# Turning the FFN's gated product with VectorE blocks and a round trip through device memory

## The chip, the cores and the metric

The kernel runs on one core of a Trainium2 chip. The metric is the device time of one execution in microseconds (us). TensorE (PE) multiplies, VectorE (DVE) and ScalarE (ACT) do elementwise work, GpSimd (POOL) has its own instruction queue, and SyncE (SP) issues the loads. Each queue can issue DMAs. The data lie in SBUF (128 partitions) and in PSUM, where TensorE writes.

## What is computed

The program is two transformer-like blocks for 256 tokens of width 2048, all in fp32. The change touches only the feed-forward part (FFN) of the first block:

```
h2 = rms_norm(x, g_pre_ffn[l]) * (1 + scale_f) + shift_f
f = (jax.nn.silu(h2 @ w_ffn_gate[l]) * (h2 @ w_ffn_up[l])) @ w_ffn_down[l]
x = x + gate_f * rms_norm(f, g_post_ffn[l])
```

`w_ffn_gate` and `w_ffn_up` are 2048 x 5632, `w_ffn_down` is 5632 x 2048. Each fp32 factor is split into a high part (rounded to the type fp32r) and a low part (the rest), and a product is the sum of three matmuls, high by high, low by high and high by low.

## The kernel before, in words

**Units and the ring.** All weights stream as *units* of 128 x 1024 fp32 (512 KB): two blocks of 128 rows by 512 columns. SP loads a unit into one of four slots of `raw`. ScalarE writes its high part to `hi` (line 572), VectorE its low part to `lo` (line 1157); both have four slots. TensorE uses a unit in 12 matmuls of 128 x 512 (lines 2002 to 2004). Semaphores tie the four: SP may refill a slot of `raw` after VectorE's `unit_split`, ScalarE may write the slot of `hi` for unit u after TensorE has finished unit u-4 (`unit_used`), and TensorE waits for `unit_split`. Each engine runs a fixed list, written by hand: in each block the call `split(n)` means "n more units of the ring", and what stands between two such calls is done there. ScalarE and VectorE may thus be up to four units ahead of TensorE.

**The FFN.** Units are counted from `FFN0` here. For each of 11 hidden tiles (512 columns of the hidden layer, `FT`) there is a *gate tile* of 8 units (accumulated in PSUM banks 0 and 1 of `acc`, one for each half of 128 tokens) and an *up tile* of 8 units (banks 2 and 3). So tile n has gate units 16n to 16n+7 and up units 16n+8 to 16n+15. When a gate tile is done, ScalarE writes its silu to `sgt` (`read_out`, line 613). When the up tile is done, VectorE multiplies it with `sgt` into `tok` (line 1726), with tokens on partitions. The down projection needs the product with hidden columns on partitions. So TensorE turns it: after unit 2 of the next gate tile (`after={1: hidden}`) it makes 8 transposes of 128 x 128 with `ident` into the PSUM banks `tb` 0 and 1 (`transpose_tok`, `transpose_pair`, line 2084), ScalarE takes the high part from there to `hidh` (`take_hi`, line 590) and VectorE the low part to `hidl` (line 1283). The turned product of the last tile is made in the same way, after unit 2 of the first down tile, by `last_hidden`, which also turns `fG` (one transpose, line 2120).

**The down projection** has 4 tiles of 22 units. Its first tile uses `hidh` and `hidl` in order of the hidden columns. Units 20 and 21 need the eleventh hidden tile (`before={FK // 2 - 2: split_now}`).

**Late modulation blocks.** During the first units of the FFN (8 to 71) the ring also carries 32 blocks of a modulation matrix, one behind every second unit, which VectorE alone uses (`late_unit`, lines 1191 and 1193). In that stretch three loads of 512 KB go through the ring for every two units.

GpSimd does a few small operations early in the program and issues no DMA. Two short DMAs on ScalarE's queue (`store_gate`, `load_gate`) carry `fG` through `gate_rows` in device memory.

Of the kernel before, what the change touches and what calls it, by code (L numbers as in the profile page):

```python
# [43 lines left out]
FT = FFN // N  # L44
# [158 lines left out]
def two_blocks(nc, x_in, fm_in, row_in, table_in, mask1_in, mask2_in, pool_in, ws_in, kidx_in,  # L203
               wa, wb, wc, out):
    with ExitStack() as ctx:
        def sem(name):
            return ctx.enter_context(nc.semaphore(name))
# [88 lines left out]
        macc_tok = sb("macc_tok", [P, UNIT], at=tok_at + TT * N * 4)  # L296
        gate_row = sb("gate_row", [KD, P])
        gate_rows = nc.dram_tensor("gate_rows", (2, KD, P), F32, kind="Internal").ap()
        end1 = top[0]
        z = sb("z", [P, TT, D], at=x_at)  # L300

# [66 lines left out]
        tr_split = sem("tr_split")  # L368
        tr_hi = sem("tr_hi")
        tr_copy = sem("tr_copy")  # L370
        u_turned = sem("u_turned")
        u_taken = sem("u_taken")
        pool_split = sem("pool_split")
# [63 lines left out]
        def part_at(part, tt):  # L437

            if part < 2:
                return k_part[:, part, tt, :]  # L440
            if part < 4:
                return v[:, tt, (part - 2) * N:(part - 1) * N]
            return z[:, tt, (part - 4) * N:(part - 3) * N]

        block = ctx.enter_context(nc.Block())

# [74 lines left out]
        @block.gpsimd  # L521
        def _(pool):
            pool.memset(ones[:], 1.0).then_inc(memory_set, 1)

            pool.wait_ge(row_loaded, 4 * 16)
            pool.memset(kT2[:], 0.0).then_inc(memory_set, 1)

            pool.affine_select(out=wsT[:], in_=wsT[:], compare_op=ALU.is_ge, fill=0.0, base=0,
                               pattern=[[0, 8], [1, P]], channel_multiplier=-1).then_inc(ws_ready, 1)

            pool.wait_ge(rstd_ready, 3)
            for tt in range(TT):
# [12 lines left out]
            pool.tensor_tensor(kr[:, :, ih:IROPE], kn[:, :, 0:ih], iropeS[:, :, ih:IROPE], ALU.mult)  # L545
            pool.tensor_copy(kd[:, :, IROPE:IDIM], kn[:, :, IROPE:IDIM])
            pool.tensor_tensor(kd[:, :, 0:IROPE], kn[:, :, 0:IROPE], iropeC[:], ALU.mult).then_inc(kn_step, 1)
            pool.wait_ge(kn_step, 4)
            pool.tensor_tensor(kd[:, :, 0:IROPE], kd[:, :, 0:IROPE], kr[:], ALU.add).then_inc(kn_step, 1)
            pool.tensor_scalar(kx[:, :, IDIM:], kx[:, :, IDIM:], IDX_SCALE, None, ALU.mult)  # L550
            pool.wait_ge(kn_step, 5)
            pool.tensor_copy(kd[:, :, IDIM:], kd[:, :, 0:IDIM]).then_inc(kidx_ready, 1)

# [4 lines left out]
        def _(act):  # L558
# [39 lines left out]
            def take_hi_tile(dst, k, gain=None):  # L598
                for b in range(2):
                    act.wait_ge(tr_split, c.up("split"))  # L600
                    take_hi(dst, k + 2 * b, b, gain and (lambda j, b=b: gain(2 * b + j)))
# [308 lines left out]
            for k in range(4, KD // 2):  # L910
                take_scaled(k)
                split(1)
            def hidden(n, first=8):
                split(first)
                tile_done()
                read_out(lambda tt: sgt[:, tt, :], 0, ACT.Silu)
                split(8)
                take_hi_tile(hidh, n * 4)

            hidden(0, FFN0 + 12 - c.n["unit"])  # L920
            for n in range(1, FFN_MOD):
                hidden(n)
            with c.loop(act, FT - FFN_MOD, unit=16, raw=16, split=2) as n:
                hidden(n + FFN_MOD)
            store_gate(1)
            split(4)
            load_gate(gm2, 1)
            for t in range(3):
                split(FK // 2 - (5 if t == 0 else 1))
                square_tile(t % 2, t)  # L930
                if t == 0:

                    load_root()
                split(1)
# [201 lines left out]
        def _(dve):  # L1136
# [581 lines left out]
                split(1)  # L1718


            def hidden(n, units=16):
                split(units - 2)
                tile_done(2)
                for tt in range(TT):

                    dve.tensor_tensor(tok[:, 0, tt, :], acc[:, 2 + tt, :], sgt[:, tt, :], ALU.mult).then_inc(acc_free[2 + tt], 1)
                split(2)
                take_lo_tile(hidl, hidh, n * 4)

            hidden(0, FFN0 + 20 - c.n["unit"])  # L1730
            for n in range(1, FFN_MOD):
                hidden(n)
            add_bias(GATE_F, KD)
            gated_gain(GATE_F, "g_post_ffn")
            with c.loop(dve, FT - FFN_MOD, unit=16, raw=16, hi=2) as n:
                hidden(n + FFN_MOD)
            for t in range(3):
                split(FK // 2 - (t == 0))
                gated_tile(fmix, gm2, t % 2, t * N)
            split(FK // 2 - RING + 1)  # L1740
            base_of(slice(0, TT))
# [241 lines left out]
        def _(pe):  # L1983
# [434 lines left out]
            keep_warm(0, 3, mergedh, mergedl)  # L2418

            def next_hidden():  # L2420
                def hidden():

                    read_out(1)
                    transpose_tok(0, tr_split)

                tile(Hh, Hl, 0, 8, after={1: hidden})
                tile(Hh, Hl, 1, 8)

            tile(Hh, Hl, 0, 8, before={k: (lambda k=k: pe.wait_ge(*split_by[k])) for k in range(KD // 2)},
# [1 line left out]
            tile(Hh, Hl, 1, 8)  # L2431
            for n in range(FFN_MOD - 1):
                next_hidden()
            with c.loop(pe, FT - FFN_MOD, unit=16, raw=16, acc0=1, acc1=1, tb0=1, tb1=1):
                next_hidden()

            def last_hidden():
                read_out(1)
                transpose_tok(0, tr_split)
                gate_rows_out(1)  # L2440

            for t in range(4):
                if t == 0:
                    tile(hidh, hidl, 0, FK // 2, before={FK // 2 - 2: split_now}, after={1: last_hidden})
                elif t < 3:
                    tile(hidh, hidl, t % 2, FK // 2)
                else:
                    tile_by_halves(hidh, hidl, 1, FK // 2)
# [259 lines left out]
```

## Time and profile before

| | |
|---|---|
| median of 3 runs | 2390.59 us (2390.33 to 2390.76) |
| the profiled execution's own time | 2391.39 us |
| its span in the trace | 2389.7 us |
| granted TensorE clock, mean | 0.999 of full speed |
| PE, DVE, ACT, POOL busy | 99%, 68%, 47%, 0% of the span |

The profile comes from one execution. Its own time stands 0.80 us above the median of the runs, and 1.7 us above its span. TensorE is busy from end to end; matmuls overlap in the trace, each lasting longer than its step, so its busy share says that it is occupied but not how fast. Times in the trace are counted from the start of the span.

### The profile page before, as it was taken

Reading aid. Unit: us, or ns where it says so; the run is one execution under the profiler, and the core shown is the slowest. Engines: PE = TensorE matmul, PEld = TensorE weight load, DVE = VectorE, ACT = ScalarE, POOL = GpSimd, SP = SyncE. Lnnn points to the kernel's source line nnn. Section 1 sums busy time; section 2 is a strip of 40 time slices with the busy share of each in tenths; the row PEclk is TensorE's granted clock in tenths of the full one; section 3 lists DMA queues with packets and bytes.
Section 4 is the critical chain, followed back from the end, with each engine's and each line's share of the span. In section 5 each row is a group of like instructions: output and inputs, shape, how many; then the busy total and the mean of one; then the engine's idle time right before and its main releaser. Section 6 shows DMA issues by size and latency. Waiting matters only on the chain.

```text
span 2389.7 us, 31107 instructions
## 1 busy us (share of the span) xinstructions
PE 2373.9 (99%) x10995; PEld 1967.1 (82%) x10995; DVE 1614.6 (68%) x1994; ACT 1120.6 (47%) x1415; POOL 9.8 (0%) x18
## 2 busy tenths in 40 slices
PE   9999999999999999999999999999999999999998
PEld 7888788888888888888888888888888888888887
DVE  7998899899787765445444465666655557777664
ACT  4544545544464444444444454445544444444554
POOL 0001000000000000000000000000000000000000
PEclk9999999999999999999999999999999999999999
DMA  9986479999857875555555556655555554444454
GB/s 392 386 314 207 152 261 353 332 340 365 308 201 259 288 252 180 196 190 185 210 193 194 194 174 204 210 203 184 193 194 193 177 195 158 151 165 157 157 189 158
DMA packets 148490, 538.54 MB, mean 225 GB/s; under 512 B 16896, under 2 KB 18208, under 8 KB 147744
## 3 DMA queue, kind: packets, MB, share of 16 engines
q1 hardware_dynamic: 145584, 528.28, 63.2%
q10 hardware_dynamic: 2800, 8.81, 1.0%
q8 instruction: 71, 1.16, 0.2%
q14 instruction: 35, 0.29, 0.0%
HBM read 534.91 MB, written 2.11 MB: 225 GB/s over the span
## 4 chain that ended last, share of the span: by engine, by line
PE 97%; DVE 1%; DMA 1%; ACT 0%; issue 0%; SPq 0%; ACTq 0%; DVEq 0%
PE acc L2002 29%; PE acc L2004 29%; PE acc L2003 29%; PE tb L2084 2%; PE tb L2534 1%; DMA start_raw<-in_wa_dram 1%; PE tb L2002 1%; PE tb L2004 0%; PE tb L2003 0%; PE acc L2054 0%; PE acc L2053 0%; PE acc L2052 0%; PE tb L2537 0%; PE tb L2271 0%; PE acc L2063 0%
## 5 line engine op out<-in xcount | busy, mean ns | idle before, releaser
L1157 DVE TENSOR_TENSOR lo<-raw,hi 128x1024 fp32r<-128x1024 f32 x809 | 968.8, 1208 | 593.4 <-ACT hi L572 590.2
L572 ACT ACTIVATE hi<-raw 128x1024 fp32r<-128x1024 f32 x809 | 842.6, 1049 | 912.4 <-PE acc L2004 722.1
L2002 PE MATMUL acc<-hi,Hh 128*128 128x512 f32 x1960 | 775.5, 396 | 1.2 <-DVE Hl L1700 0.7
L2004 PE MATMUL acc<-hi,Hl 128*128 128x512 f32 x1960 | 764.3, 390 | 0.0
L2003 PE MATMUL acc<-lo,Hh 128*128 128x512 f32 x1960 | 763.1, 389 | 0.0
L2002 PEld LDWEIGHTS acc<-hi,Hh 128*128 128x128 f32 x1960 | 368.1, 188 | 79.2 <-issue 4.6
L2004 PEld LDWEIGHTS acc<-hi,Hl 128*128 128x128 f32 x1960 | 367.8, 188 | 77.9
L2003 PEld LDWEIGHTS acc<-lo,Hh 128*128 128x128 f32 x1960 | 368.3, 188 | 75.6 <-issue 1.4
L2002 PE MATMUL acc<-hi,hbh 128*128 128x512 f32 x512 | 204.7, 400 | 0.0
L2004 PE MATMUL acc<-hi,hbl 128*128 128x512 f32 x512 | 200.1, 391 | 0.0
L2003 PE MATMUL acc<-lo,hbh 128*128 128x512 f32 x512 | 199.6, 390 | 0.0
L2002 PE MATMUL acc<-hi,hidh 128*128 128x512 f32 x336 | 130.8, 389 | 0.0
L2004 PE MATMUL acc<-hi,hidl 128*128 128x512 f32 x336 | 130.7, 389 | 0.0
L2003 PE MATMUL acc<-lo,hidh 128*128 128x512 f32 x336 | 130.7, 389 | 0.0
L1193 DVE SCALAR_TENSOR_TENSOR macc<-late_raw,fm,macc 128x1024 f32<-128x1024 f32 x90 | 114.9, 1277 | 0.4
L2004 PEld LDWEIGHTS acc<-hi,hbl 128*128 128x128 f32 x512 | 96.1, 188 | 20.6
L2003 PEld LDWEIGHTS acc<-lo,hbh 128*128 128x128 f32 x512 | 96.4, 188 | 18.5
L2002 PEld LDWEIGHTS acc<-hi,hbh 128*128 128x128 f32 x512 | 96.3, 188 | 18.1
L2004 PEld LDWEIGHTS acc<-hi,hidl 128*128 128x128 f32 x336 | 63.1, 188 | 13.2
L2003 PEld LDWEIGHTS acc<-lo,hidh 128*128 128x128 f32 x336 | 63.1, 188 | 13.0
L2002 PEld LDWEIGHTS acc<-hi,hidh 128*128 128x128 f32 x336 | 63.1, 188 | 13.0
L1330 DVE SCALAR_TENSOR_TENSOR macc<-start_raw,fm,macc 128x1024 f32<-128x1024 f32 x45 | 57.5, 1278 | 0.1
(338 smaller groups left out, 1970.5 us busy)
## 6 DMA issues: line engine op xcount, KB each, us to landing
raw<-in_wa_dram SPq DMA_DIRECT2D x680, 512.0 KB, 4.3
late_raw<-in_wa_dram SPq DMA_DIRECT2D x96, 512.0 KB, 5.4
raw<-in_wb_dram SPq DMA_DIRECT2D x96, 512.0 KB, 4.2
start_raw<-in_wa_dram SPq DMA_DIRECT2D x64, 512.0 KB, 7.7
raw<-in_wc_dram SPq DMA_DIRECT2D x64, 512.0 KB, 3.5
x<-in_x_dram SPq DMA_DIRECT2D x2, 1024.0 KB, 6.1
gm<-gate_rows ACTq DMA_DIRECT2D x2, 1024.0 KB, 9.0
x<-in_x_dram ACTq DMA_DIRECT2D x1, 2048.0 KB, 9.3
```

Source lines behind the costliest of these rows:

```text
L572: act.activation(hi[:, s, 0:n], raw[:, r, 0:n], ACT.Copy).then_inc(hi_ready, 1)
L1157: dve.tensor_tensor(lo[:, s, 0:n], raw[:, r, 0:n], hi[:, s, 0:n].bitcast(F32), ALU.subtract)\
L1193: ins = dve.scalar_tensor_tensor(dst, w, vec("c", kt), dst, ALU.mult, ALU.add)
L1330: ins = dve.scalar_tensor_tensor(dst, start_raw[s][:], vec("c", kt), dst, ALU.mult, ALU.add)
L2002: pe.matmul(dst(tt), a, hi[:, s, w], start=first and i == 0, stop=False)
L2003: pe.matmul(dst(tt), a, lo[:, s, w], start=False, stop=False)
L2004: mm = pe.matmul(dst(tt), b, hi[:, s, w], start=False, stop=last and i == kts - 1)
L2084: ins = pe.transpose(tb[:, b, j * T + tt * P:j * T + (tt + 1) * P], src(tt, j), ident[:])
L2534: pe.matmul(tb[:, g // 2, (g % 2) * T:(g % 2 + 1) * T], q(g, P, P), k(T), start=True, stop=True)
```

## The change

TensorE's 88 transposes of the gated product go, and so do ScalarE's and VectorE's reads of `tb`. In their place:

1. VectorE, right behind the product, transposes it in 32 x 32 blocks (two instructions, one for each half of the tokens) from `tok` into `sgt`, whose silu is spent by then. The blocks are so placed that partition 32i+c holds block row c of token block i.
2. GpSimd stores the 512 KB of `sgt` to the new device tensor `hid_rows`, waits until that has landed, and reads it back in four DMAs of 32 partitions x 4 x 256 elements (128 KB each) into `tok`. The moves between groups of 32 partitions happen in these reads. Every run of bytes is 4 KB in the store and 1 KB in the reads.
3. ScalarE makes `hidh` from `tok` (`hidden_hi`) late in the next gate tile: behind its split of unit 16n+27, ahead of that gate tile's silu. VectorE makes `hidl` (`hidden_lo`) behind its split of the same unit.
4. For the last tile both happen at unit 12 of the first down tile. TensorE waits there for `hid_split` ahead of unit 0 (for the tenth tile) and ahead of unit 20 (for the eleventh).

The transpose of `fG` stays. The diff, cut to its core:

```
+            for n in range(FT):
+                pool.wait_ge(hid_blocks, n + 1)
+                pool.dma_start(hid_rows[:, :, :], blocks_out).then_inc(hid_stored, 16)
+                pool.wait_ge(hid_stored, 16 * (n + 1))
+                for j in range(4):
+                    pool.dma_start(blocks_in[32 * j:32 * j + 32, :, :], hid_rows[:, j, :].rearrange("(i c) m -> c i m", i=4))\
+                        .then_inc(hid_turned, 16)
...
-            def hidden(n, first=8):
-                split(first)
+            def hidden_hi(n, turned):
+
+                act.wait_ge(hid_turned, turned)
+                for tt in range(TT):
+                    act.activation(hidh[:, cols(n * 4, 4), tt * P:(tt + 1) * P].rearrange("p k (i t) -> p k i t", i=4),
+                                   turned_half(tt), ACT.Copy).then_inc(hid_hi, 1)
+
+            def hidden(n, turned):
+                split(16)
+                hidden_hi(n, turned)
                 tile_done()
                 read_out(lambda tt: sgt[:, tt, :], 0, ACT.Silu)
-                split(8)
-                take_hi_tile(hidh, n * 4)
...
+            def hidden_lo(n, taken):
+
+                for tt in range(TT):
+                    dve.wait_ge(hid_hi, taken + tt + 1)
+                    at = slice(tt * P, (tt + 1) * P)
+                    four = lambda ap: ap.rearrange("p k (i t) -> p k i t", i=4)
+                    ins = dve.tensor_tensor(four(hidl[:, cols(n * 4, 4), at]), turned_half(tt),
+                                            four(hidh[:, cols(n * 4, 4), at].bitcast(F32)), ALU.subtract)
+                ins.then_inc(hid_split, 1)
+
+            def hidden(units=6):
+                split(units)
                 tile_done(2)
                 for tt in range(TT):
-
                     dve.tensor_tensor(tok[:, 0, tt, :], acc[:, 2 + tt, :], sgt[:, tt, :], ALU.mult).then_inc(acc_free[2 + tt], 1)
-                split(2)
-                take_lo_tile(hidl, hidh, n * 4)
...
+                for tt in range(TT):
+                    ins = dve.transpose(blocks_out[:, :, tt * P:(tt + 1) * P].rearrange("p j (k t) -> p j k t", k=4),
+                                        tok[:, 0, tt, :].rearrange("p (k j c) -> p j k c", k=4, j=4))
+                ins.then_inc(hid_blocks, 1)
+                split(10)
...
-                def hidden():
-
-                    read_out(1)
-                    transpose_tok(0, tr_split)
-
-                tile(Hh, Hl, 0, 8, after={1: hidden})
+                tile(Hh, Hl, 0, 8)
                 tile(Hh, Hl, 1, 8)
...
-                    tile(hidh, hidl, 0, FK // 2, before={FK // 2 - 2: split_now}, after={1: last_hidden})
+                    tile(hidh, hidl, 0, FK // 2, before={i: (lambda n=n: pe.wait_ge(hid_split, n)) for i, n in ((0, FT - 1), (FK // 2 - 2, FT))},
+                         after={1: lambda: gate_rows_out(1)})
```

How the lists of the engines change shows at three places. The numbers at a row's start are the engine's count of instructions, and waits stand in brackets. First TensorE behind unit 2 of the second gate tile, before the change:

```order
2960 L2003 MATMUL acc<-lo,Hh 128x512
2961 L2004 MATMUL acc<-hi,Hl 128x512
2962 L2084 MATMUL tb<-ident,tok 128x128 [waits tb_free0,acc_free3,acc_free2]
2963 L2084 MATMUL tb<-ident,tok 128x128 x3
2964 L2084 MATMUL tb<-ident,tok 128x128 [waits tb_free1]
2965 L2084 MATMUL tb<-ident,tok 128x128 x3
2966 L2002 MATMUL acc<-hi,Hh 128x512 [waits unit_split]
```

With the change the rows of line 2084 are gone there, and the matmuls of the next unit follow directly. Next VectorE, from the product of the first hidden tile on, before:

```order
755 L1726 TENSOR_TENSOR tok<-acc,sgt 128x512 [waits unit_used]
756 L1726 TENSOR_TENSOR tok<-acc,sgt 128x512
757 L1193 SCALAR_TENSOR_TENSOR macc_end<-raw,fm,macc_end 128x1024 [waits raw_loaded3,unit_split]
758 L1157 TENSOR_TENSOR lo<-raw,hi 128x1024 [waits hi_ready] x2
759 L1283 TENSOR_TENSOR hidl<-tb,hidh 128x512 [waits tr_hi] x2
760 L1193 SCALAR_TENSOR_TENSOR macc_end<-raw,fm,macc_end 128x1024 [waits raw_loaded2,unit_split]
761 L1157 TENSOR_TENSOR lo<-raw,hi 128x1024 [waits hi_ready] x2
```

and VectorE at the same place with the change:

```order
755 L1767 TENSOR_TENSOR tok<-acc,sgt 128x512 [waits unit_used]
756 L1767 TENSOR_TENSOR tok<-acc,sgt 128x512
757 L1773 STREAM_TRANSPOSE sgt<-tok 128x4x128 [waits acc_free3,acc_free2]
758 L1773 STREAM_TRANSPOSE sgt<-tok 128x4x128
759 L1225 SCALAR_TENSOR_TENSOR macc_end<-raw,fm,macc_end 128x1024 [waits raw_loaded3,unit_split]
760 L1189 TENSOR_TENSOR lo<-raw,hi 128x1024 [waits hi_ready] x2
761 L1225 SCALAR_TENSOR_TENSOR macc_end<-raw,fm,macc_end 128x1024 [waits raw_loaded2,unit_split]
762 L1189 TENSOR_TENSOR lo<-raw,hi 128x1024 [waits hi_ready] x2
```

The two transposes now stand directly behind the product, and the low part (`hidl`) has moved ten units down, to instruction 769. Last, ScalarE at the end of the second gate tile with the change (the silu `sgt<-acc` stood there before too, and `hidh` eight units further up):

```order
431 L593 ACTIVATE hi<-raw 128x1024 [waits unit_used,raw_loaded0]
432 L593 ACTIVATE hi<-raw 128x1024 [waits unit_used,raw_loaded1]
433 L938 ACTIVATE hidh<-tok 128x4x128 [waits hid_turned]
434 L938 ACTIVATE hidh<-tok 128x4x128
435 L634 ACTIVATE sgt<-acc 128x512 [waits unit_used]
436 L634 ACTIVATE sgt<-acc 128x512
437 L593 ACTIVATE hi<-raw 128x1024 [waits unit_used,raw_loaded3]
```

ScalarE's wait for the four reads (`hid_turned`) now stands ahead of the silu and of the split of the next unit.

## Rows read from the trace of the kernel before

**Rows 1.** The page: busy time by engine.
```profile
PE 2373.9 (99%) x10995; PEld 1967.1 (82%) x10995; DVE 1614.6 (68%) x1994; ACT 1120.6 (47%) x1415; POOL 9.8 (0%) x18
```

**Rows 2.** The page: chain that ended last, share of the span by line.
```profile
PE acc L2002 29%; PE acc L2004 29%; PE acc L2003 29%; PE tb L2084 2%; PE tb L2534 1%; DMA start_raw<-in_wa_dram 1%; PE tb L2002 1%; PE tb L2004 0%; PE tb L2003 0%; PE acc L2054 0%; PE acc L2053 0%; PE acc L2052 0%; PE tb L2537 0%; PE tb L2271 0%; PE acc L2063 0%
```

**Rows 3.** Two stretches of the FFN: busy us and counts, clock, DMA share, GB/s.
```profile
core 0: us, PE busy (x) PEld busy (x) DVE busy (x) ACT busy (x) POOL busy (x), PEclk, DMA share, GB/s
688.00:863.00 175.00, 175.00 (x793) 145.19 (x792) 124.56 (x116) 75.16 (x81) 0.00 (x0) 1.00 0.80 277
863.00:1164.00 301.00, 301.00 (x1358) 249.66 (x1357) 148.55 (x138) 127.91 (x136) 0.00 (x0) 1.00 0.57 194
```

**Rows 4.** PE timeline around the transposes of the second hidden tile: start, duration, engine, line.
```profile
766.92 0.39 PE L2004 MATMUL acc<-hi,Hl 128*128 128x512 f32 x1
767.15 1.03 PE L2084 MATMUL tb<-ident,tok 128*128 128x128 f32 x8
767.94 0.48 PE L2002 MATMUL acc<-hi,Hh 128*128 128x512 f32 x1
768.26 0.40 PE L2003 MATMUL acc<-lo,Hh 128*128 128x512 f32 x1
768.49 0.39 PE L2004 MATMUL acc<-hi,Hl 128*128 128x512 f32 x1
```

**Rows 5.** PE timeline, last hidden tile, with the transpose of fG.
```profile
1163.49 0.39 PE L2002 MATMUL acc<-hi,hidh 128*128 128x512 f32 x1
...
1168.71 0.40 PE L2004 MATMUL acc<-hi,hidl 128*128 128x512 f32 x1
1168.94 1.04 PE L2084 MATMUL tb<-ident,tok 128*128 128x128 f32 x8
...
1169.84 0.48 PE L2002 MATMUL acc<-hi,hidh 128*128 128x512 f32 x1
1170.16 0.40 PE L2003 MATMUL acc<-lo,hidh 128*128 128x512 f32 x1
1170.39 0.39 PE L2004 MATMUL acc<-hi,hidl 128*128 128x512 f32 x1
```

**Rows 6.** All groups of PE, by shape: busy us, mean ns, idle before.
```profile
L2084 PE MATMUL tb<-ident,tok 128*128 128x128 f32 x400 | 51.9, 272 | 0.7 <-DVE tok L1275 0.7
```

**Rows 7.** VectorE timeline from the second product on, idle time in brackets.
```profile
761.91 1.29 DVE L1726 TENSOR_TENSOR tok<-acc,sgt 128x512 f32<-128x512 f32 x2 [1.21 <-PE acc L2004]
...
768.42 1.29 DVE L1283 TENSOR_TENSOR hidl<-tb,hidh 128x512 fp32r<-128x512 f32 x2 [1.76 <-ACT hidh L590]
769.62 1.27 DVE L1193 SCALAR_TENSOR_TENSOR macc_end<-raw,fm,macc_end 128x1024 f32<-128x1024 f32 x1
770.82 2.35 DVE L1157 TENSOR_TENSOR lo<-raw,hi 128x1024 fp32r<-128x1024 f32 x2
```

**Rows 8.** ScalarE timeline at the end of the second gate tile.
```profile
742.58 1.07 ACT L572 ACTIVATE hi<-raw 128x1024 fp32r<-128x1024 f32 x1 [0.34 <-DMA raw<-in_wa_dram]
743.54 1.06 ACT L613 ACTIVATE sgt<-acc 128x512 f32<-128x512 f32 x2
746.40 1.06 ACT L572 ACTIVATE hi<-raw 128x1024 fp32r<-128x1024 f32 x1 [1.80 <-DMA raw<-in_wa_dram]
```

**Rows 9.** Instructions that write or read tok: ns min/median/max, first and last start.
```profile
L1275 DVE TENSOR_TENSOR tok<-tok,sgt x44: 413/682/694, 210.8 to 2199.2; 128x512 f32<-128x512 f32 x40, 128x256 f32<-128x256 f32 x4
L1010 ACT ACTIVATE x<-tok x8: 617/625/635, 1638.6 to 1707.8; 128x512 f32 x8
```

**Rows 10.** The page: DMA issues, KB each, median us from issue to landing.
```profile
raw<-in_wa_dram SPq DMA_DIRECT2D x680, 512.0 KB, 4.3
late_raw<-in_wa_dram SPq DMA_DIRECT2D x96, 512.0 KB, 5.4
start_raw<-in_wa_dram SPq DMA_DIRECT2D x64, 512.0 KB, 7.7
```

**Rows 11.** Waits in the stretch 688 to 1164 us: total us, times, longest.
```profile
ACT hi L572 <- PE acc L2004: 143.5, 93, 2.2
ACT hi L572 <- DMA raw<-in_wa_dram: 85.7, 53, 4.2
```

More of the change, by code:

```diff
@@ L298, in two_blocks @@
         gate_rows = nc.dram_tensor("gate_rows", (2, KD, P), F32, kind="Internal").ap()
+        hid_rows = nc.dram_tensor("hid_rows", (P, 4, TT * P), F32, kind="Internal").ap()
         end1 = top[0]
@@ L370, in two_blocks @@
         tr_copy = sem("tr_copy")
+        hid_blocks = sem("hid_blocks")
+        hid_stored = sem("hid_stored")
+        hid_turned = sem("hid_turned")
+        hid_hi = sem("hid_hi")
+        hid_split = sem("hid_split")
         u_turned = sem("u_turned")
@@ L443, in part_at, with turned_half @@
             return z[:, tt, (part - 4) * N:(part - 3) * N]
+        blocks_out = sgt[:].rearrange("p a (j m) -> p (a j) m", j=2)
+        blocks_in = tok[:, 0].rearrange("p a (i m) -> p (a i) m", i=2)
+        def turned_half(tt):
+            return blocks_in[:, :, tt * P:(tt + 1) * P].rearrange("p i (k t) -> p k i t", k=4)
         block = ctx.enter_context(nc.Block())
@@ L912, in _ @@
                 split(1)
-            def hidden(n, first=8):
-                split(first)
+            def hidden_hi(n, turned):
[6 more added lines that the diff above has]
+                hidden_hi(n, turned)
                 tile_done()
                 read_out(lambda tt: sgt[:, tt, :], 0, ACT.Silu)
-                split(8)
-                take_hi_tile(hidh, n * 4)
[L920 to L924, printed above, removed]
+            split_to(FFN0 + 12)
+            tile_done()
+            read_out(lambda tt: sgt[:, tt, :], 0, ACT.Silu)
+            for n in range(FFN_MOD - 1):
+                hidden(n, 64 * (n + 1))
+            with c.loop(act, FT - FFN_MOD, unit=16, raw=16) as n:
+                hidden(n + (FFN_MOD - 1), n * 64 + 64 * FFN_MOD)
+            split(8)
             store_gate(1)
@@ L927, in _ @@
             load_gate(gm2, 1)
+            split(4)
+            hidden_hi(FT - 1, 64 * FT)
             for t in range(3):
-                split(FK // 2 - (5 if t == 0 else 1))
+                split(FK // 2 - (9 if t == 0 else 1))
                 square_tile(t % 2, t)
@@ L1718, in _ @@
                 split(1)
-            def hidden(n, units=16):
-                split(units - 2)
+            def hidden_lo(n, taken):
[8 more added lines that the diff above has]
+                split(units)
                 tile_done(2)
@@ L1726, in hidden @@
                     dve.tensor_tensor(tok[:, 0, tt, :], acc[:, 2 + tt, :], sgt[:, tt, :], ALU.mult).then_inc(acc_free[2 + tt], 1)
-                split(2)
-                take_lo_tile(hidl, hidh, n * 4)
-            hidden(0, FFN0 + 20 - c.n["unit"])
+                n = c.up("hidden")
+                for tt in range(TT):
+                    dve.wait_ge(acc_free[2 + tt], n + (TILES_BEFORE_OUT // 2 + 3))
+                for tt in range(TT):
+                    ins = dve.transpose(blocks_out[:, :, tt * P:(tt + 1) * P].rearrange("p j (k t) -> p j k t", k=4),
+                                        tok[:, 0, tt, :].rearrange("p (k j c) -> p j k c", k=4, j=4))
+                ins.then_inc(hid_blocks, 1)
+                split(10)
+            hidden(FFN0 + 18 - c.n["unit"])
             for n in range(1, FFN_MOD):
-                hidden(n)
+                hidden_lo(n - 1, TT * (n - 1))
+                hidden()
             add_bias(GATE_F, KD)
             gated_gain(GATE_F, "g_post_ffn")
-            with c.loop(dve, FT - FFN_MOD, unit=16, raw=16, hi=2) as n:
-                hidden(n + FFN_MOD)
+            with c.loop(dve, FT - FFN_MOD, unit=16, raw=16, hidden=1) as n:
+                hidden_lo(n + (FFN_MOD - 1), n * TT + TT * (FFN_MOD - 1))
+                hidden()
+            hidden_lo(FT - 1, TT * (FT - 1))
             for t in range(3):
-                split(FK // 2 - (t == 0))
+                split(FK // 2 - (9 if t == 0 else 0))
                 gated_tile(fmix, gm2, t % 2, t * N)
@@ L2433, in _ @@
                 next_hidden()
-            with c.loop(pe, FT - FFN_MOD, unit=16, raw=16, acc0=1, acc1=1, tb0=1, tb1=1):
+            with c.loop(pe, FT - FFN_MOD, unit=16, raw=16, acc0=1, acc1=1):
                 next_hidden()
[L2437 to L2440, printed above, removed]
             for t in range(4):
                 if t == 0:
-                    tile(hidh, hidl, 0, FK // 2, before={FK // 2 - 2: split_now}, after={1: last_hidden})
+                    tile(hidh, hidl, 0, FK // 2, before={i: (lambda n=n: pe.wait_ge(hid_split, n)) for i, n in ((0, FT - 1), (FK // 2 - 2, FT))},
+                         after={1: lambda: gate_rows_out(1)})
                 elif t < 3:
```

## Prediction

> **What bounds the kernel now.** I read the page first. TensorE is busy for 99% of the span, VectorE for 68%, ScalarE for 47%, GpSimd for almost nothing [rows 1]. The chain of waits that ended last runs through the matmuls of the weight stream (lines 2002 to 2004, 29% each), and the transposes of line 2084, those of every stage together, hold 2% of it [rows 2]. So nothing but TensorE's own list sets the end, and an instruction taken off that list is worth its step in the list, as long as no wait takes its place. Then I read the FFN by stretches [rows 3]: full clock in both, TensorE without a gap, DMA queues 80% busy while the late modulation blocks share the ring (688 to 863 us) and 57% afterwards. VectorE works 124.56 of 175 us in the first. Last I read timelines around one hidden tile for the steps and the leads.
>
> **A step of TensorE.** From the first matmul at 1163.49 to the one at 1168.71 there are 23 steps [rows 5], so a matmul costs 0.227 us of TensorE's time although each lasts 0.39, and a unit of 12 costs 2.72 us.
>
> **What is removed.** In the second hidden tile the last matmul ahead of the transposes starts at 766.92, and the second behind them at 768.26 [rows 4]. That is 1.34 us where two steps would be 0.45. The 8 transposes cost 0.89 us, 0.11 each. In the last tile the same distance is 1168.71 to 1170.16, 1.45 us, with the transpose of fG among them [rows 5]: 1.00 us for nine, again 0.11 each. All 11 tiles: 11 x 0.89 = **9.8 us**. Bounds: fG's transpose stays and is alone now; if it then costs a whole duration (0.272 us by the mean in [rows 6]) and not 0.11, the gain is 9.6. The busy time in [rows 6] gives 51.9 / 400 = 0.130 us for one transpose, and 88 of them 11.4 us, the upper end. I take 9.8, since it is the measured distance between matmuls. The Trainium skill (VectorE: DVE Perf Modes, The three transpose paths) puts TensorE's 128x128 transpose at 390 ns, measured in bf16, and its rules for kernel authors say to turn 128x128 on TensorE when PSUM will do; by that figure the estimate would be 34.3 us gained, and by that rule no change of this kind. The trace disagrees with the figure as a price: transposes overlap, and only the step is paid.
>
> **What is added to VectorE.** Two block transposes of 128 x 512 behind the product. No row shows one; the nearest is an operation of the same size in SBUF, 0.682 us [rows 9], so 1.36 us for both, between 0.82 (two of the 0.413 of half the size) and 2.4 (two like the split of 1024 columns, 2.35 for a pair [rows 7]). The low part stays two operations (1.29 before [rows 7], 1.36 from SBUF). Four tiles add some 6 us to the 124.56 of 175 in the busiest stretch [rows 3]. It is hidden by VectorE's lead. That lead is least right here: unit 34 starts at 767.94 and is 0.09 us longer than 2.72 [rows 4], so TensorE starts unit 36 at 773.5. Its low part is the first of the two that start at 770.82, and ends at 772.0 [rows 7]. The lead is 1.5 us, because both engines stood for the transposes (VectorE idle for 1.76 us, and its 1.29 us of work). This stop goes away, and the 1.36 us of block transposes come in its place. So the least lead should grow, not shrink. If the cover were gone, four tiles by 1.36 us would be 5.4 us.
>
> **What is added to ScalarE.** The high part from SBUF: two of 0.625 us [rows 9] ahead of the silu. Before, ScalarE stood idle 1.80 us after that silu, waiting for a weight load [rows 8]; the 1.25 us fit in it. The split of the next unit does not move. VectorE's low part delays the modulation block behind it by about 1.3 us and so refills that ring slot later; the lead takes it.
>
> **What is added to the queues.** GpSimd issues five DMAs for each tile; nothing is queued behind them but the next tile's. SP's list is unchanged. Each tile moves 1.05 MB more. At 277 GB/s for a share of 0.80 [rows 3] the queues do 346 GB/s when full, so this is 3.0 us of their time. In some 10 us of such a trip they have 2.0 us to spare in the first stretch, so the loads fall behind by about 1.0 us, or 2.5 if the reads cost double for their runs of 1 KB. Afterwards the share is 0.57 and there is room.
>
> **When the turned tile lands.** Call T the end of an up tile. The product starts at once and takes 1.29 us [rows 7], the transposes 1.36. Store: a load of the same 512 KB takes 4.3 us, 5.4 or 7.7 with company [rows 10]. I take 5.4. The four reads have 512 KB together: 4.3 if they run side by side like one load, four times as long if one after the other. I take 7.7, side by side, with the issues and short runs. Landing at T + 15.8 us (T + 11.3 at best). ScalarE asks for it at the end of the gate tile, T + 21.8 (8 units), so there is no wait. TensorE would stand only if it were later still: it wants unit 28 at T + 32.6, and behind the landing lie the high part 1.25, silu 1.06, a split 1.06 [rows 8] and VectorE's 1.2. So **T + 28.0** is where a late trip begins to cost.
>
> **At the end.** TensorE's wait ahead of the first down tile is for the tenth tile, done some 20 us before. The eleventh is wanted at unit 20 of the down tile, 54 us after T. Neither costs.
>
> **Sum.** 2391.39 - 9.8 = 2381.6 for an execution like the profiled one. The median of the runs is 0.8 lower: 2390.59 - 9.8 = **2380.8 us**.
>
> **Rivals.**
> 1. *The round trip is late, and the kernel is slower.* GpSimd's DMAs have no row here: it issued none. If the reads go one after the other, 5.4 us each, the tile lands at T + 2.7 + 5.4 + 21.6 = T + 29.7, and ten gate tiles stand 1.7 us each: 2380.8 + 17 = 2398 us. It decides from 5.0 us a read on, at a store of 5.4. Against it: a read has a quarter of the bytes, and nothing makes the second wait for the first. Chance 0.06.
> 2. *GpSimd is held up by VectorE.* If each of the five issues must wait until a stretch of VectorE's work like the 2.35 us in [rows 7] is over, 11.8 us are added: T + 27.6, just not late, so still 2380.8; but with the store at 7.7 it is T + 29.9 and 1.9 us x 10, which is 2400 us. The Trainium skill (SBUF — State Buffer, SBUF: two separate sides) warns that a GpSimd DMA starves while VectorE runs an operation that takes both ports. Its page VectorE: DVE Perf Modes (Walkthrough: the 8-slice pipeline in each mode) says that an operation on two tensors never does so, as the split's subtraction is. No row here shows the effect. Chance 0.04.
> 3. *The ring runs dry beside the modulation blocks.* Four tiles lie there. If the backlog of 2.5 us is not covered by the lead, up to 10 us: 2381 to 2391, middle 2386. For it: ScalarE already waited 53 times and 85.7 us for loads in the FFN [rows 11]. Against it: most of its waiting, 143.5 us, is for TensorE, and the lead loses its stop. Chance 0.12.
> 4. *The gain isn't there, or something fixed is paid for GpSimd's DMAs.* If TensorE's time comes back elsewhere the result is 2390.6. A fixed price of the size of what lies around the span now, 1.7 us, would give 2382.5. Chance 0.05 for the first.
>
> **Numbers.** The forecast has the remaining 0.73. Its own range is 2379.0 (11.4 gained, rounded down) to 2382.7 (9.6 gained, 1.7 paid). To hold 8 in 10 it needs the better half of the third rival: 2379.0 to 2387.0. What a measurement of this kernel can tell from no change is about 0.2%, 4.8 us, so faster means below 2385.8. The forecast and half of the third rival give 0.80, and I add 0.02 for the mild ends of the first two. Same, 0.11: the other half and the fourth. Slower, 0.07.
>
> **What would show it.** Right: no transposes in the FFN on TensorE; two units on either side 2.72 us apart; the four reads landing before the gate tile ends; ScalarE never waiting there; TensorE's idle time unchanged. Wrong: a gap on TensorE at unit 28 of a tile (rivals 1 and 2), or gaps at units 18 to 22 of the first four tiles (rival 3), or block transposes beyond 1.2 us each.

## The result, and the profile after

| | before | changed |
|---|---|---|
| median | 2390.72 us (13 runs, 2390.16 to 2392.68) | 2396.27 us (13 runs, 2389.64 to 2400.09) |
| ratio | | 1.0022, 95% interval 1.0015 to 1.0029 |
| profiled execution | 2391.39 us, span 2389.7 | 2389.64 us, span 2387.9 |

The changed kernel is slower by about 5 us, and it scatters over 10 us where the kernel before keeps within 2.5. The forecast was 2380.8 us, in a range of 2379.0 to 2387.0. The profiled execution is the fastest of the 13, so its trace shows the mechanism and too little of the harm; a second profile of the same kernel further down shows the rest.

The page of the changed kernel, busy time by engine (compare [rows 1]), then three of its groups with their idle time behind the second bar:

```profile
PE 2364.3 (99%) x10907; PEld 1957.9 (82%) x10907; DVE 1628.8 (68%) x2016; ACT 1121.4 (47%) x1415; POOL 40.2 (2%) x73
...
L1189 DVE TENSOR_TENSOR lo<-raw,hi 128x1024 fp32r<-128x1024 f32 x809 | 970.0, 1208 | 612.0 <-ACT hi L593 609.3
L593 ACT ACTIVATE hi<-raw 128x1024 fp32r<-128x1024 f32 x809 | 843.3, 1049 | 954.2 <-PE acc L2055 735.5
L2053 PE MATMUL acc<-hi,Hh 128*128 128x512 f32 x1960 | 775.5, 396 | 8.5 <-DVE lo L1189 7.3
```

TensorE has 88 instructions fewer, as planned, and works 9.6 us less. But its matmuls now stand idle for 8.5 us, 7.3 of them for VectorE's low part. The two stretches of the FFN, for comparison with [rows 3]:

```profile
688.00:863.00 175.00, 170.36 (x750) 139.33 (x749) 125.69 (x119) 72.00 (x76) 10.62 (x19) 1.00 0.86 291
863.00:1164.00 301.00, 298.32 (x1320) 246.59 (x1319) 160.15 (x154) 131.35 (x140) 17.00 (x32) 1.00 0.68 220
```

4.6 us of idle time on TensorE lie in the first stretch, beside the modulation blocks. The 2.7 us of the second lie at its very start, at unit 70, where the last of these blocks stands. In the whole FFN there are five gaps between matmuls above 0.6 us, at 733.03, 772.23, 779.22, 825.23 and 870.96, of 0.85, 1.64, 1.58, 2.08 and 3.06 us. Less one step each they make 8.1 us. The stretch from the first matmul with `Hh` to the first with `hidh` takes 492.3 us before (671.22 to 1163.49) and 492.6 with the change (670.87 to 1163.44). So the ten sets of transposes that are gone there, 8.9 us, are all eaten, 8.1 us by the five gaps and the rest by shorter waits. The profiled execution is 1.7 us faster than that of the kernel before all the same: 0.85 us come from the eleventh set, in the down projection, 0.35 us from an earlier start of this stretch, and 0.8 us from stages behind the down projection that the change doesn't touch. That 9.8 - 8.1 gives 1.7 too is chance.

What led to the gap at 772.23 is seen on VectorE (timeline, idle time in brackets; compare [rows 7]):

```profile
761.83 1.28 DVE L1767 TENSOR_TENSOR tok<-acc,sgt 128x512 f32<-128x512 f32 x2
763.21 1.31 DVE L1773 STREAM_TRANSPOSE sgt<-tok 128x512 f32<-128x512 f32 x2
764.44 1.24 DVE L1225 SCALAR_TENSOR_TENSOR macc_end<-raw,fm,macc_end 128x1024 f32<-128x1024 f32 x1
765.60 2.35 DVE L1189 TENSOR_TENSOR lo<-raw,hi 128x1024 fp32r<-128x1024 f32 x2
767.87 1.28 DVE L1225 SCALAR_TENSOR_TENSOR macc_end<-raw,fm,macc_end 128x1024 f32<-128x1024 f32 x1
772.59 2.50 DVE L1189 TENSOR_TENSOR lo<-raw,hi 128x1024 fp32r<-128x1024 f32 x2 [3.44 <-ACT hi L593]
```

The line at 765.60 is the pair of low parts of units 34 and 35. The same pair in the kernel before:

```profile
764.31 2.35 DVE L1157 TENSOR_TENSOR lo<-raw,hi 128x1024 fp32r<-128x1024 f32 x2
```

And TensorE with the change (timeline):

```profile
766.45 0.39 PE L2055 MATMUL acc<-hi,Hl 128*128 128x512 f32 x1
766.88 0.50 PE L2053 MATMUL acc<-hi,Hh 128*128 128x512 f32 x1
...
772.23 0.39 PE L2055 MATMUL acc<-hi,Hl 128*128 128x512 f32 x1
773.87 0.50 PE L2053 MATMUL acc<-hi,Hh 128*128 128x512 f32 x1 [1.25 <-DVE lo L1189]
```

The block transposes take 0.69 us each, as costed. But they stand ahead of the low part of unit 34, the first of the pair at 765.60. It ends at 766.8, and TensorE starts that unit at 766.88, 0.2 us late. So the lead was gone before the reads of this tile's trip were issued (the first at 769.20). Part of it had not come back since the trip of the tile before: for unit 32 it was 1.3 us, and 2.3 in the kernel before. The block transposes took the rest. In the kernel before the lead at unit 34 was 2.4 us (765.5 to 767.94), 0.8 of them TensorE's own transposes ahead of that unit; 1.4 us of block transposes leave 0.2 of it even without any trip. Behind it ScalarE waited for a load (timeline):

```profile
765.01 1.06 ACT L593 ACTIVATE hi<-raw 128x1024 fp32r<-128x1024 f32 x1 [0.20 <-DMA raw<-in_wa_dram]
771.50 1.06 ACT L593 ACTIVATE hi<-raw 128x1024 fp32r<-128x1024 f32 x1 [5.43 <-DMA raw<-in_wa_dram]
```

That load landed at 771.47, and in the kernel before the one for the same unit landed at 767.83. It was issued 1.3 us later (765.86, before 764.56), since VectorE freed the slot later, and took 5.6 us where it took 3.3. The stretches around the trips show what it met. First the kernel before, then the changed one (the last three numbers are clock, DMA share and GB/s):

```profile
725.00:735.00 10.00, 10.00 (x46) 8.27 (x45) 7.74 (x8) 3.48 (x4) 0.00 (x0) 1.00 0.74 268
770.00:780.00 10.00, 10.00 (x46) 8.28 (x45) 7.48 (x7) 3.19 (x3) 0.00 (x0) 1.00 0.82 282
```

```profile
725.00:735.00 10.00, 9.54 (x43) 7.58 (x42) 5.69 (x5) 4.24 (x4) 1.05 (x2) 1.00 1.02 342
770.00:780.00 10.00, 8.35 (x36) 6.27 (x34) 4.13 (x4) 3.18 (x3) 1.38 (x3) 1.00 1.01 315
```

In both of these stretches the DMA queues are full for 10 us. The page's issues of the trip:

```profile
hid_rows<-sgt POOLq DMA_DIRECT2D x11, 512.0 KB, 3.2
tok<-hid_rows POOLq DMA_DIRECT2D x44, 128.0 KB, 6.1
```

A read of a quarter of the bytes takes twice as long as the store. How much of that comes from the full queues and how much from the runs of 1 KB is not shown. The weight load issued at 769.33, in the middle of the four reads of that tile, took 9.1 us to land, and the gap at 779.22 follows from it; in the kernel before, loads around such a place (710 to 745 us) took 3.1 to 5.8.

### The profile page after: what moved, and what is told of

It reads as the page before. It is cut to its first block, busy times and chain, and to the rows that moved or that the text cites. A ratio compares the mean times of both kernels' runs of the same rounds, so it can differ in the third digit from the quotient of the medians.

```text
span 2387.9 us, 30997 instructions
## 1 busy us (share of the span) xinstructions
PE 2364.3 (99%) x10907; PEld 1957.9 (82%) x10907; DVE 1628.8 (68%) x2016; ACT 1121.4 (47%) x1415; POOL 40.2 (2%) x73
## 4 chain that ended last, share of the span: by engine, by line
PE 92%; DMA 4%; DVE 3%; ACT 1%; issue 0%; SPq 0%; ACTq 0%; DVEq 0%
PE acc L2053 28%; PE acc L2055 28%; PE acc L2054 28%; DMA raw<-in_wa_dram 3%; PE tb L2135 2%; PE tb L2576 1%; DVE lo L1189 1%; DMA start_raw<-in_wa_dram 1%; ACT hi L593 1%; PE tb L2053 1%; PE tb L2054 0%; PE tb L2055 0%; PE acc L2105 0%; PE acc L2104 0%; PE acc L2103 0%
## 5 line engine op out<-in xcount | busy, mean ns | idle before, releaser
L2053 PEld LDWEIGHTS acc<-hi,Hh 128*128 128x128 f32 x1960 | 368.2, 188 | 89.4 <-DVE lo L1189 11.4
L2053 PEld LDWEIGHTS acc<-hi,hbh 128*128 128x128 f32 x512 | 96.3, 188 | 18.2
```

Of the source, the lines that this page charges most:

```text
L2053: pe.matmul(dst(tt), a, hi[:, s, w], start=first and i == 0, stop=False)
```

## The experiments

Theory A: the ring runs dry beside the modulation blocks, because the block transposes use up its lead and the trip delays the loads. Rival B: GpSimd's DMAs have a price of their own, in every tile or once. Each kernel was timed with runs of the kernel before on the same chip, whose medians lay between 2390.45 and 2390.89 us. The ratios below are to these.

### Where it is lost: only the late tiles by the new way

```
-            for n in range(FT):
+            for n in range(FT - 4):
                 pool.wait_ge(hid_blocks, n + 1)
...
             for n in range(FFN_MOD - 1):
-                next_hidden()
+                next_hidden(True)
```

with the old take of `hidh` and `hidl` for tiles 0 to 3.

> The first four hidden tiles, those beside the modulation blocks, are turned on TensorE as before; the other seven go by VectorE's blocks and GpSimd's round trip. Theory A (the loss is made beside the modulation blocks alone, where the ring has too little lead for the block transposes and the extra traffic): no gap on TensorE in the FFN, 7 x 0.89 = 6.2 us gained, about 2384.5 us, and runs as close together as before. Rival B (GpSimd's queue costs something wherever it is used: a fixed price, or VectorE and GpSimd hindering each other in every tile): seven elevenths of the loss remain, 2390 to 2394 us, with the same scatter.

Measured: 2384.24 us (2383.94 to 2385.18, 7 runs), ratio 0.9972 (0.9961 to 0.9984). Theory A's number. Seven tiles gain their 0.89 us each and lose nothing, though a late tile fills the queues just as much:

```profile
905.00:915.00 10.00, 10.00 (x46) 8.27 (x45) 4.03 (x5) 4.24 (x4) 1.34 (x3) 1.00 1.00 310
```

Share 1.00 here where the kernel before has 0.60, and TensorE still works 10.00 of 10 us. There is no fixed price: rival B is out as a price of every tile or of the launch.

### What it is made of: blocks, trip, or neither

Without the trip (and in the last of the three also without the transposes):

```
-                pool.dma_start(hid_rows[:, :, :], blocks_out).then_inc(hid_stored, 16)
-                pool.wait_ge(hid_stored, 16 * (n + 1))
-                for j in range(4): ...
+                pool.sem_inc(hid_turned, 64)
```

> The changed kernel with its block transposes but without the store and the four reads; GpSimd only passes the signal on, and ScalarE and VectorE take the product as it lies, so the hidden layer is not turned. Theory A, if the extra traffic is the larger part: the least lead is about that at unit 18 in the changed kernel, 0.4 us, gaps are rare or none, 2381 to 2383 us. If VectorE's 1.4 us behind the product are the larger part: gaps at units 18 to 22 of the first four tiles remain, 2384 us or more. Rival B gives 2381 too, if it is the DMAs.

Without the block transposes:

```
-                for tt in range(TT):
-                    ins = dve.transpose(...)
-                ins.then_inc(hid_blocks, 1)
+                dve.sem_inc(hid_blocks, 1)
```

> The changed kernel with the store and the four reads but without VectorE's block transposes: the old silu is stored and read back, so the product is not used. Theory A: the lead at unit 18 of a tile is 1.4 us larger than in the changed kernel, the reads still delay the loads; fewer and shorter gaps, 2382 to 2388 us. If the round trip alone makes the loss, the time is that of the changed kernel, 2389 to 2400 us.

> The changed kernel without block transposes and without the round trip; the hidden layer is not turned. All theories: TensorE's list is shorter by 88 transposes and nothing new is in the way, so the whole 9.8 us are gained, 2380.9 us, with no gap in the FFN and runs within 1 us of each other. A smaller gain would mean that the transposes' price was read wrongly.

Measured: neither, 2380.47 us (2380.1 to 2382.57, 4 runs, ratio 0.9958, 0.9941 to 0.9974), so the price of the transposes on TensorE was right. Blocks alone 2381.95 us (2380.1 to 2383.34, 5 runs), trip alone 2389.78 us (2386.54 to 2395.62, 10 runs), both 2396.27. For the trip alone theory A had said 2382 to 2388 us: the trip costs more by itself than it allowed, though less than the whole loss. From 2380.5 the blocks alone cost 1.5 us, the trip alone 9.3, both together 15.8, which is 5 us more than their sum (3.9 with the 2395.14 us of the changed kernel's second measurement, below). That is how a shared reserve behaves: the blocks alone leave almost all of TensorE's steps untouched (one idle time of 0.2 us in that trace), the trip alone breaks through (six gaps, 0.73 to 2.47 us), and with the reserve already used by the blocks more of the trip's delay lands on TensorE. The ranges of blocks alone and neither overlap, so the 1.5 us are hardly told from nothing. The excess over the sum is uncertain too: by resampling the runs its 95% interval is 1.6 to 8.9 us, and with the second measurement -0.1 to 7.1. Part of it may also be the clock, which in some executions was lower behind a long gap (below). The reserve itself can be read where the trip is left out (VectorE, then TensorE, timeline):

```profile
766.68 2.35 DVE L1185 TENSOR_TENSOR lo<-raw,hi 128x1024 fp32r<-128x1024 f32 x2
768.14 0.39 PE L2049 MATMUL acc<-hi,Hh 128*128 128x512 f32 x1
```

The low part of unit 34 ends at 767.9, and TensorE starts the unit at 768.14. So the block transposes alone take the lead there from 2.4 us to 0.2.

### The reserve itself: the modulation blocks spread out

```
-FFN_MOD = 5
+FFN_MOD = 9
...
-... + spaced(FFN0 + 8, 64, 32)
+... + spaced(FFN0 + 8, 120, 32)
```

> The changed kernel with its 32 modulation blocks spread over 120 units of the FFN (one behind about every fourth unit) and not 64 (every second). Nothing else differs. Theory A (the ring's lead beside the blocks is what runs out): the lead between the blocks grows, no gap or one or two short ones, 2381 to 2383 us, the best version so far, and runs close together. If GpSimd's traffic hurts by itself, the gaps spread to eight tiles and the time stays at 2390 or above.

> The kernel before, with TensorE's transposes, and its 32 modulation blocks spread over 120 units. It has no gap on TensorE in the FFN to begin with, so more lead buys nothing: 2390.6 us, the same within 0.5. If the spreading itself gained time, the gain of the version that spreads and uses the round trip would be partly due to it.

Measured: the changed kernel with spread blocks takes **2382.19 us** (2381.54 to 2383.75, 6 runs), ratio 0.9965 (0.9953 to 0.9978). All 11 tiles go through GpSimd's round trip, and two gaps of 1.18 and 0.86 us are left. The kernel before with the same spreading takes 2390.52 us, ratio 0.9999 (0.9990 to 1.0008): it had no gap to lose. So 13 to 14 us of the changed kernel's time hang on where 32 loads stand, and in the kernel before nothing does. Of all runs this pair speaks most directly for theory A. The loads are not spared in it: between 688 and 863 us the slowest takes 10.2 us from issue to landing with the spread blocks, 9.2 in the changed kernel and 6.6 in the kernel before. So the gain doesn't come from faster loads.

### What in the trip hurts: bytes, time or burst

Store without reads (`pool.sem_inc(hid_turned, 64)` in place of the four reads):

> The changed kernel with the block transposes and the store, without the four reads (the hidden layer is not turned). Half of the extra bytes, in runs of 4 KB. If the bytes count: half the harm, 2384 to 2389 us. If it is the reads with their runs of 1 KB, four in flight beside the loads: nearly all the harm goes, 2381.5 to 2383.5 us.

The whole trip later:

```
                 pool.wait_ge(hid_blocks, n + 1)
+                pool.wait_ge(unit_used, RING + FFN0 + 16 * n + 20)
```

> The changed kernel, but GpSimd starts each store only when TensorE has finished unit 4 of the next gate tile (about T + 11 instead of T + 2.7), so that the traffic does not fall on the place where VectorE's product and block transposes have just used up the lead. The tile lands about T + 23, inside the T + 28 allowed. If the coincidence makes the gaps: 2383 to 2388 us. If the ring beside the modulation blocks has no room for the traffic at any time: about as the changed kernel, 2392 to 2398 us.

The trip on ScalarE's queue:

```
             def hidden(n, turned, blocks, stored):
-                split(16)
+                split(8)
+                store_hidden(blocks)
+                split(2)
+                load_hidden(stored)
+                split(6)
                 hidden_hi(n, turned)
```

> The changed kernel with the store and the four reads issued on ScalarE's queue, between its splits, and not on GpSimd's. Same bytes, same runs. If the loss comes from bytes and lead, the time is like the changed kernel's, 2390 to 2400 us. If it comes from the way GpSimd's DMAs are made or served, the gaps go and the time is 2381 to 2384 us.

GpSimd's reads at the time at which ScalarE's queue had them (the line added for the later trip, but ahead of the reads):

> The changed kernel with GpSimd's four reads held back until TensorE has finished unit 3 of the next gate tile, about where ScalarE's queue issued them in the run with that queue; the store stays where it was. If that run's gain of 7 us over the changed kernel came from the time of the reads: 2388 to 2390 us here. If it came from the queue: 2393 to 2397 us here.

The block transposes two units later (`split(2)` ahead of them, `split(8)` behind, where `split(10)` was):

> The changed kernel with VectorE's two block transposes two units later (behind the split of unit 16n+19 and not directly behind the product). The slots of the ring beside the product come free 1.4 us earlier, and the trip starts some 5 us later. If the transposes' place right behind the product matters: lead at unit 18 about 1.8 us instead of 0.4, fewer gaps, 2384 to 2390 us. If only the traffic matters: about as the changed kernel or the one with a later trip, 2391 to 2397 us.

| kernel | median us (runs) | range | ratio (interval) |
|---|---|---|---|
| store only | 2383.84 (10) | 2381.38 to 2387.42 | 0.9971 (0.9962 to 0.9981) |
| whole trip later | 2392.37 (10) | 2389.97 to 2394.9 | 1.0008 (0.9999 to 1.0018) |
| ScalarE's queue | 2389.18 (10) | 2388.36 to 2391.28 | 0.9994 (0.9985 to 1.0004) |
| reads held back | 2390.75 (10) | 2388.73 to 2393.7 | 1.0002 (0.9992 to 1.0011) |
| transposes later | 2387.35 (10) | 2386.03 to 2390.96 | 0.9988 (0.9978 to 0.9997) |

The store with the blocks costs 3.4 us above 2380.5, and adding the reads takes that to 15.8, with as many bytes again. So it is mostly the reads; the two answers that I had set against each other (half the harm, nearly none) both missed, the value lies at the edge between them. Moving the transposes away from the place where the lead is least brings 8.9 us of the loss back. It also moves the reads to 11.4 us behind the start of the product, the time at which they start when held back, so the transposes' place by itself is worth the 3.4 us between those two kernels. Moving the trip alone brings 3.9; its 2392.37 us lies in the range that I had given for "no room for the traffic at any time", and not in 2383 to 2388. Holding back the reads alone brings 5.5. (With the second measurement each is 1.1 us less.) All three are in the direction of theory A, that two disturbances at one place cost more than the same two apart, but the later trip says also that it costs most of its price wherever it stands beside the modulation blocks. It landed later than expected as well, 23.7 to 29.6 us behind the start of the product, and ScalarE waited for it in the tiles behind the modulation blocks; the matmuls of the down projection take 0.6 us more than in the changed kernel. Nothing of this kind reaches the version with the spread blocks.

ScalarE's queue gives 2389.18 where GpSimd's at about the same time gives 2390.75. Each lies 0.8 us outside the range that I had named for it. So most of its 7 us over the changed kernel is a matter of when the reads start; the 1.6 us that are left may be the queue, but the ranges of the two overlap. The Trainium skill (DMA: Bandwidth & Descriptors, Issuing engines are not separate DMA queues) says that DMAs from all issuing engines run on the same 16 DMA engines and interleave, so that another queue saves only the issuing time. These two runs don't contradict it.

### The same chip, the same bytes, one read at a time

The changed kernel had been timed on another chip than its variants, so it was run again beside this one:

```
                         .then_inc(hid_turned, 16)
+                    pool.wait_ge(hid_turned, 64 * n + 16 * (j + 1))
```

> The changed kernel once more, on the same chip as the next run. On the first chip it took 2396.3 us and scattered over 10 us, while kernels with the same bytes took 2389 to 2392 us on other chips. If the size of the loss belongs to the program: 2394 to 2398 us here too. If it is a matter of the chip or of chance: 2390 to 2393 us, and the differences of some us between the versions of the round trip beside the modulation blocks may not be read.

> The changed kernel with each of GpSimd's four reads issued only when the one before has landed. The same bytes and runs, never more than one read in flight, so the traffic is thinner and lasts longer; the tile lands later, about T + 20, still inside T + 28. If the burst of four reads together is what delays the loads: gaps fewer and shorter, 2386 to 2391 us. If only the sum of bytes and the ring's lead count: as the changed kernel on the same chip.

Measured: the changed kernel 2395.14 us (2391.49 to 2398.91, 11 runs), ratio 1.0011 (1.0002 to 1.0020); one read at a time 2389.28 us (2385.86 to 2391.72, 11 runs), ratio 0.9990 (0.9981 to 0.9999). The loss belongs to the program and not to a chip, and 5.9 us of it go when the four reads are no longer in flight at once. The slowest weight load between 688 and 863 us now takes 6.7 us, where it took 9.8 beside it, and the median read takes 4.7 us, where it took 6.3. The stretch at 725 us shows the thinner traffic:

```profile
725.00:735.00 10.00, 10.00 (x45) 8.17 (x44) 6.17 (x6) 4.25 (x4) 0.66 (x2) 1.00 0.94 320
```

The share is 0.94 and TensorE has no gap there (1.02 and 9.54 of 10 in the changed kernel). Six gaps are left, 0.72 to 1.84 us. Four of them (1.17, 1.80, 1.31 and 1.08 us) lie elsewhere, 32 to 34 us behind the start of the product, at unit 28 of each of the first four tiles, since the trip now takes so long: the last read of the second tile lands at 793.4, T + 31 or so, which is behind the T + 28.0 of the prediction, and not at the T + 20 that I had expected. ScalarE shows the wait (timeline):

```profile
793.44 1.16 ACT L939 ACTIVATE hidh<-tok 128x512 fp32r<-128x512 f32 x2 [4.02 <-DMA tok<-hid_rows]
```

So this kernel pays the price of rival 1, a late trip, as well, and the 5.9 us are what is left of the gain after it.

The second profile of the changed kernel (span 2397.2 us) is the slowest of its 11 executions, and shows what the fastest one hid. TensorE's timeline around its gap beside the second trip:

```profile
779.99 0.39 PE L2055 MATMUL acc<-hi,Hl 128*128 128x512 f32 x1
783.57 0.50 PE L2053 MATMUL acc<-hi,Hh 128*128 128x512 f32 x1 [3.19 <-DVE lo L1189]
783.91 0.48 PE L2054 MATMUL acc<-lo,Hh 128*128 128x512 f32 x1
784.19 0.63 PE L2055 MATMUL acc<-hi,Hl 128*128 128x512 f32 x1
784.62 0.63 PE L2053 MATMUL acc<-hi,Hh 128*128 128x512 f32 x1
...
787.17 0.54 PE L2053 MATMUL acc<-hi,Hh 128*128 128x512 f32 x1
787.56 0.40 PE L2054 MATMUL acc<-lo,Hh 128*128 128x512 f32 x1
```

and two stretches behind gaps (clock third from the end):

```profile
880.00:886.50 6.50, 5.90 (x15) 4.64 (x16) 4.22 (x4) 3.49 (x4) 0.00 (x0) 0.50 0.64 222
...
784.10:787.50 3.40, 3.40 (x9) 2.62 (x8) 2.78 (x3) 1.62 (x2) 0.00 (x0) 0.50 0.73 245
788.00:792.00 4.00, 4.00 (x21) 3.37 (x20) 2.51 (x2) 0.57 (x1) 0.00 (x0) 1.00 0.80 305
```

The gap of 3.58 us between matmuls is followed by 3.4 us with a granted clock of 0.50, the lower of the two levels (1.2 GHz instead of 2.4). The steps there are 0.43 us instead of 0.227. The gap of 3.66 us at 876.93 goes with 6.8 us at 0.50, from 879.7 on, 0.9 us before its next matmul starts. From the first matmul with `Hh` to the first with `hidh` this execution takes 501.4 us, and that of the kernel with neither blocks nor trip 483.2: 18.2 us lost. Its four gaps above 0.6 us, less their steps, are 11.7 us. The 10.2 us at the lower level, less the 0.9 in which TensorE stood still, cost about half, 4.6 us. The remaining 1.9 us are shorter waits and the longer first steps behind gaps. So a gap costs itself, and in some executions the slow steps behind it too. That is part of the scatter.

### The best version

The spread blocks with the trip on ScalarE's queue:

> The version with spread modulation blocks, with the store and the four reads on ScalarE's queue. The version with GpSimd's queue has two short gaps left (0.95 and 0.63 us) and 2382.2 us. If ScalarE's queue disturbs the loads less, the gaps go: 2380.8 to 2381.5 us. If the queue makes no difference there: 2382 to 2382.5 us.

Measured: **2380.82 us** (2380.43 to 2381.29, 5 runs), ratio 0.9959 (0.9945 to 0.9972). No gap is left in its FFN, and its two stretches have TensorE busy throughout:

```profile
688.00:863.00 175.00, 175.00 (x777) 144.86 (x776) 113.18 (x108) 75.69 (x81) 0.00 (x0) 1.00 0.79 264
863.00:1164.00 301.00, 301.00 (x1333) 249.08 (x1333) 179.00 (x172) 131.73 (x141) 0.00 (x0) 1.00 0.73 242
```

DMA share and VectorE's work are now nearly even over the two. This is the whole 9.8 us that the transposes were worth, and the fastest kernel of the study that computes the result. It is also 1.4 us faster than the same with GpSimd's queue, and the ranges don't overlap, as I had expected if ScalarE's queue disturbs the loads less. But its reads also start 0.9 us later in most of the first tiles and its store lands 0.5 us sooner (2.7 and 3.2 us), and the two ran on different chips. What makes the 1.4 us stays open.

## Why the prediction was wrong

- *What bounds the kernel, and the price of a step*: right. 88 transposes are worth 9.8 us; the kernel with neither blocks nor trip gained 10.4 (2390.89 to 2380.47), and the best version 9.6 (2390.45 to 2380.82).
- *Durations*: block transposes 0.69 us each (0.68 assumed), the store 3.2 to 4.1 us (5.4 assumed), a read 6.1, and all four together 9.5 in the second tile (7.7 assumed). The second tile landed at 778.7, T + 16.9 where T + 15.8 was forecast: it is that near because a store costed too long and reads costed too short offset each other. ScalarE never waited for it. Rivals 1 and 2, the late trip, did not occur in the changed kernel.
- *"The least lead should grow, not shrink"*: this is the step that failed. I looked for the least lead behind the old take (1.5 us at unit 36) and saw that this stop goes away. But the block transposes stand earlier, ahead of the low part of unit 34, which the old stop never delayed. The order rows in the text above show it: line 1773 lies between the product and the first split, line 1283 lay behind two splits. The lead at unit 34 goes from 2.4 us to 0.2 by the blocks alone, and with the trip of the tile before it is gone: TensorE starts 0.2 us late. The pair of low parts that began at 764.31 in the kernel before began at 765.60. The late modulation block and both ring slots behind it came free 1.3 us later too. I put a cost against a relief at another place.
- *"The loads fall behind by about 1.0 us, or 2.5"*: mis-sized. I spread the bytes over 10 us and subtracted a mean spare share. In fact the queues were full for those 10 us (1.02 and 1.01), single loads took up to 9.1 us in place of 3.1 to 5.8, and the delayed slot went round: a load that lands late is split late, so the next load into that slot is issued late.
- *Rival 3, the ring running dry*, was the case that occurred. It had a chance of 0.12 and a ceiling of 10 us. Measured against 2380.5 its price is 15.8. Two things were left out: that the lead is spent by the blocks before the trip comes, and that TensorE's clock was lower behind long gaps in some executions. My list of signs named "gaps at units 18 to 22 of the first four tiles", and that is where they came: units 22, 36, 38, 54 and 70 of the FFN are units 22, 20, 22, 22 and 22 counted from each tile's start.
- *The chances*: 0.82 for faster rested on leads read at one unit of one tile. That the best version takes the 2380.8 us of the forecast doesn't bear out the part that failed: it was reached by moving the modulation blocks.

## What to carry to other kernels

A transfer or an operation that is "hidden" lives on a reserve: measure the lead of the feeder over the bottleneck at each unit that the new work stands ahead of, not at the worst unit of the old program. Where a burst of DMAs meets a ring that is already 80% busy, price it by the landing times it causes and not by the mean share, and split the burst or move the competing loads apart. Here it took only the placing of 32 loads to turn a loss of 5 us into a gain of 8 to 10.

## What was not expected of the hardware

- In the profiles of the round trip's versions the granted clock was 0.50 for 3.4 or 6.8 us after gaps of 2.3 to 3.7 us between matmuls (2.30 with the transposes later, 2.47 without them, 2.49 with the reads held back, 3.65 with the later trip, in which TensorE makes four transposes near the end, 3.58 and 3.66 in the second profile of the changed kernel), and stayed at 1.00 after others as long (2.30, 2.59, 3.06, 3.11). What decides between them was not tried.
- The store costs 1.9 us (2381.95 to 2383.84, with ranges that overlap), and four reads of 128 KB in runs of 1 KB, issued within 1.6 us, another 11 to 12 us for the same 512 KB. Whether the short runs or the four at once matter more was tried only for the second (5.9 us); reads with longer runs were not tried.
